# Stick-breaking attention beside weight pieces: another order of a head's steps on ScalarE and VectorE

## The reference

```python
z = einsum(q, k) / sqrt(128)                       # queries of block n, keys 0..(n+1)*128-1
ln = where(before, log_sigmoid(-z), 0)             # before: strictly causal
within = ln @ tri_within                           # reverse exclusive sums inside a 128-key chunk
after = sums of later chunks
w = where(before, exp(z + ln + within + after), 0)
out = w @ v
yb = out @ w_branch_b                              # later: gate_a * ya + gate_b * yb, then w_out
```

## Time and profile before

| | |
|---|---|
| median of three runs | 3065.51 us |
| the profiled execution | 3064.16 us, span 3062.4 us |
| PE busy | 2972.5 us, 97% |
| DVE busy | 1933.2 us, 63% |
| ACT busy | 1523.7 us, 50% |
| mean granted clock of PE | 0.99 |
| DMA | 178 GB/s mean |

### The profile page before, as it was taken

How to read it: one execution, slowest core, us unless ns; L and a number is a source line. 1 busy time by engine, 2 the same in 40 slices (tenths; PEclk the granted TensorE clock), 3 DMA queues, 4 the chain that set the end, 5 groups by cost and what they waited for, 6 DMA issues and landing times. The chain is left out here.

```text
span 3062.4 us, 49424 instructions
## 1 busy us (share of the span) xinstructions
PE 2972.5 (97%) x17246; PEld 2590.4 (85%) x17246; DVE 1933.2 (63%) x2197; ACT 1523.7 (50%) x1897; POOL 265.4 (9%) x217
## 2 busy tenths in 40 slices
PE   7999999999999999999999998999799999999979
PEld 6788888988888888888888887988688888888867
DVE  6487665556665656556656665565777567657664
ACT  4485554444544444444544456444466455545544
POOL 3010011102101010000200000001300000010131
PEclk9999999999999999999999999999899999999989
DMA  7555557665566666665665544655365666656544
GB/s 213 161 160 171 160 169 219 183 179 180 187 195 186 192 192 188 190 189 181 195 186 176 165 152 141 188 168 176 118 188 179 192 192 187 186 185 188 173 130 158
DMA packets 544862, 544.80 MB, mean 178 GB/s; under 512 B 17032, under 2 KB 543880, under 8 KB 544752
## 3 DMA queue, kind: packets, MB, share of 16 engines
q1 hardware_dynamic: 543200, 539.42, 57.8%
q0 software_dynamic: 1552, 3.97, 0.4%
HBM read 541.23 MB, written 2.10 MB: 177 GB/s over the span
## 5 line engine op out<-in xcount | busy, mean ns | idle before, releaser
L1234 DVE TENSOR_TENSOR w_low<-raw,w_high 128x1024 fp32r<-128x1024 f32 x1024 | 1266.7, 1250 | 867.8 <-ACT w_high L895 861.1
L596 PE MATMUL ps_gemm<-act_a,w_high 128*128 128x512 f32 x4480 | 1584.8, 399 | 43.7 <-DVE w_low L1234 25.8
L895 ACT CAST w_high<-raw 128x1024 fp32r<-128x1024 f32 x1024 | 1056.5, 1044 | 1025.0 <-PE ps_gemm L598 1006.6
L598 PE MATMUL ps_gemm<-act_a,w_low 128*128 128x256 f32 x4640 | 1302.9, 281 | 0.0
L596 PE MATMUL ps_gemm<-act_b,w_high 128*128 128x512 f32 x3264 | 1150.2, 398 | 6.3 <-DVE act_b L1243 4.7
L596 PEld LDWEIGHTS ps_gemm<-act_a,w_high 128*128 128x128 f32 x4480 | 846.4, 189 | 252.0 <-issue 41.4
L598 PE MATMUL ps_gemm<-act_b,w_low 128*128 128x256 f32 x3520 | 984.4, 280 | 0.0
L598 PEld LDWEIGHTS ps_gemm<-act_a,w_low 128*128 128x128 f32 x4640 | 882.4, 190 | 0.1
L596 PEld LDWEIGHTS ps_gemm<-act_b,w_high 128*128 128x128 f32 x3264 | 614.2, 188 | 153.6 <-issue 6.0
L598 PEld LDWEIGHTS ps_gemm<-act_b,w_low 128*128 128x128 f32 x3520 | 665.3, 189 | 0.2
L1268 DVE TENSOR_TENSOR summ<-ps_gemm,bcopy 128x512 f32<-128x512 f32 x228 | 156.0, 684 | 22.0 <-ACT bcopy L911 21.4
(11 more groups left out here) (247 smaller groups left out, 1192.1 us busy)
## 6 DMA issues: line engine op xcount, KB each, us to landing
raw<-in_w_in SPq DMA_DIRECT2D x352, 512.0 KB, 4.3
raw<-in_w_up SPq DMA_DIRECT2D x176, 512.0 KB, 3.5
raw<-in_w_mlp_up SPq DMA_DIRECT2D x128, 512.0 KB, 3.9
raw<-in_w_mlp_down SPq DMA_DIRECT2D x128, 512.0 KB, 4.3
raw<-in_w_down SPq DMA_DIRECT2D x88, 512.0 KB, 4.3
raw<-in_w_out SPq DMA_DIRECT2D x64, 512.0 KB, 4.5
raw<-in_w_branch SPq DMA_DIRECT2D x32, 512.0 KB, 4.5
raw<-in_w_ple_gate SPq DMA_DIRECT2D x32, 512.0 KB, 4.4
```

The source lines that it names most:

```text
L596: nc.tensor.matmul(ps[:, g, t, :], wh[:, at, o:o + P], x, start=first, stop=False, skip_group_check=True)
L598: last = nc.tensor.matmul(ps[:, g, t, 0:S], wl[:, at, o:o + P], high(x), start=False, stop=final, skip_group_check=True)
L895: nc.scalar.copy(wh[:, at, 0:kn * S], raw[:, at, 0:kn * S]).then_inc(high_ready, 1)
L1234: nc.vector.tensor_tensor(wl[:, at, 0:kn * S], raw[:, at, 0:kn * S], wh[:, at, 0:kn * S].bitcast(F32), ALU.subtract).then_inc(split_done, 1)
```

## The change

ACT and DVE do more steps of a head directly one behind another, with fewer pieces and no gate epilogue between them; the fillers move behind the head. The Sigmoid table is loaded ahead of the wait for `scaled` in the epilogues of gates_b0, and the load of the Exp table ahead of the second Exp goes (the set natural_log_exp_and_others, loaded for Ln, holds it). The query of the next head is scaled at the end of a head. On PE the loop's first three pieces stand before the loop and again at its end, which leaves its order of instructions as it was; only the value awaited before mix_b0's even pieces is another.

```diff
+            take(fill, 3)
             for h in range(SLOTS):
-                take(fill, 3)
                 pe.wait_ge(y_high, 20 + h)
...
                                  skip_group_check=True).then_inc(s_o, 1)
+                take(fill, 3)
             take(fill)
...
                 def need_y2(i, j, s):
-                    pe.wait_ge(y_done, 24)
+                    pe.wait_ge(y_done, 24 if j % 2 else 20)
...
                 if k == "gate":
+                    if ph.name == "gates_b0":
+                        nc.scalar.preload_act_table(ACT.Sigmoid)
                     act.wait_ge(scaled, after("scaled", ph, i, j))
...
+            take(fill, 2)
             for h in range(SLOTS):
 
-                take(fill, 3)
                 nc.scalar.preload_act_table_set("natural_log_exp_and_others")
...
                 take(fill, 3)
-                nc.scalar.preload_act_table(ACT.Exp)
                 act.wait_ge(s_logw, h + 1)
                 nc.scalar.activation(w3, w3, ACT.Exp).then_inc(s_w, 1)
                 take(fill, 2)
...
                 nc.scalar.copy(act_a[:, 4 + h, 0:S], PJ[:, 28, :]).then_inc(y_high, 1)
+                take(fill, 3)
             take(fill)
...
-            for h in range(SLOTS):
+            take(fill, 2)
+
+            def scale_q(h):
+
                 dve.wait_ge(y_done, 20 + h)
                 nc.vector.tensor_scalar(PJ[:, 20, :], G[:, h, :], HD2_SCALE, None, ALU.mult).then_inc(s_q, 1)
-                take(fill, 2)
+            scale_q(0)
+            for h in range(SLOTS):
                 dve.wait_ge(s_z, h + 1)
...
                 nc.vector.tensor_copy(PJ[:, 21, :], pm[:, 2, 0:S]).then_inc(s_v, 1)
-                take(fill, 2)
                 dve.wait_ge(s_lnb, h + 1)
...
                 nc.vector.tensor_tensor(w3, z3, pm[:, 1, 0:3 * P], ALU.add).then_inc(s_logw, 1)
-                take(fill, 2)
+                take(fill, 3)
                 dve.wait_ge(y_high, 20 + h + 1)
                 low(act_a[:, 4 + h:5 + h, :], PJ[:, 28:29, :], y_done)
+                if h + 1 < SLOTS:
+                    scale_q(h + 1)
+                take(fill, 3)
             take(fill)
```

## The result

The changed kernel took 3043.14 us (median of 19 runs, 3036.70 to 3057.59), the kernel before on the same chip 3062.87 (19 runs, 3056.04 to 3082.54): ratio 0.9936, 95% interval 0.9921 to 0.9950, a gain of 19.7 us (15 to 24). The forecast was 3050 with a range of 3045 to 3060. The profiled execution has a span of 3043.9 us against 3062.4.

A forecast was written before the change was run, and what follows sets the result against it. TensorE, 97% busy, was taken as the bound, so only its stops and lower clock could be won: -12.9 (stops) + 0.25 (query 0) - 3.1 (clock) = -15.75 us, giving 3050 us against the median; range 3045 to 3060.

The forecast's parts named there:

- the last step of the sum: -15.75 us on the profiled 3064.16 gives 3048.4; 1.35 added for the median of 3065.51 gives 3050 us.
- Steps 1 to 5: ACT and DVE order within a head: PE's stops before suffix sums and output go, head 1 becomes 24.6 us.
- Step 3: Masks on DVE ahead of two w_low: the stop before the suffix sums goes, 1.24 us a head.
- step 5: DVE addition and second Exp ahead of the gate epilogue, no Exp table: stop before output goes, 2.41 us.
- step 1: Gate epilogue on ACT: Sigmoid table loaded before the wait for DVE, so Sigmoid ends by 1833.5.
- Step 7: Scaling of query 0 ahead of the first scores: PE waits for it, +0.25 us once (0 to 0.7).
- Step 8: mix_b0 waits for 20 instead of 24 on even pieces: 0 on both sides.
- Step 9: Loads of raw pieces land in 3.6 us, about 7 us available: ACT does not come to wait for one.
- The clock: Stick-breaking stretch: both falls of the granted clock behind output stops of heads 2 and 3 go, 3.1 us (0 to 3.1).
- the clock falls anyway: Rival: the clock falls at other places of the stretch, giving 3053 us; chance 0.15.
- The rival of the thin cover: Fifth piece's w_low, slack 1.5 us, comes late and PE stops there: gain partly given back, 3057 to 3059; chance 0.20.

The follow-up runs named there:

- experiment with three loads: Three more table loads (3.87 us) per head on ACT ahead of the Ln steps, against the changed kernel; 3057.36 us, ratio 0.9981 to the kernel before.

## Why the prediction fell short

The time lies outside the range though every stop went as forecast. What failed is the last step of the sum, the one that sets it "against the median", and the range that was put on it.

- **Steps 1 to 5, order and stops: right.** Head windows of 24.6 were forecast and measured. The stage gives 16.3 us in the first pair of profiles against 12.9 + 3.1 = 16.0 for stops and clock, and 15.6 by the means of all profiles.
- **How the gain divides over the steps: wrong.** Step 3 gave the masks 1.24 us a head, step 5 the Exp 2.41. Alone, the masks are worth 0.75 us a head (28.44 to 27.7), and the Exp step alone is worth 3.6 to 3.8 (28.44 to 24.88 and 24.63), which is all there is. That the sum of the two held is luck in part: both edits were made, and the second would have done it without the first. The table load ahead of the wait (step 1) had been named as what makes Ln early; it is needless.
- **Step 7: right**, 0.25 us. **Step 8: right**, nothing. **Step 9: right**, ACT waits for no load, though the DMA share rose from 0.48 to 0.55.
- **The clock: right**, and firmer than the chance of 0.15 for "the clock falls anyway" had it: 9 falls in five profiles of before, none in the five of the changed order. A fall costs 1.6 us: the stage is 230.8 with one and 232.5 with two. What the prediction held against it, that the clock stayed up behind the stops of head 1, was chance of that one profile: in the third and fifth it fell there.
- **The term that failed is the base.** The sum of -15.75 us was put on the median of three runs, 3065.51; 71 runs put it at 3062.2. With that base the forecast would have been 3046.4, and the range, moved down by the same 3.3 us, would have held the result.
- **What the sum put at nothing.** The other 3 us to the 3043.4 of all changed runs are the excess of the time over the stage. The prediction let the rest of the program stand as it was, without a reason; the profiles show it to differ by up to 17 us between executions of one kernel (1015.7 to 1032.9 behind the stage), and the cause of the 3 us is not found.
- **The range was too narrow for both.** It came from the bounds of the terms and from three runs 8 us apart. Runs of either kernel have a standard deviation near 6 us. A part of it is the pace of PE's pairs, which differs by 2% and is another in each execution. Another part goes with the clock: 6 of the 52 runs of before with a clock on record have a mean of 0.988 or less, and they are its slowest or nearly so, 3070.1 to 3081.0 us against a mean of 3061.3 for the others. Where in those runs the clock is lost no profile shows.
- **The rival of the thin cover: did not come**, at 1.4 us of cover. The experiment with three loads shows that it was the right place, and that a delay beyond the cover is paid in full.

## What to carry over

When two stops in one loop end with different instructions, don't add their lengths as the worth of two edits: look on each engine for the one block (here a gate epilogue, waited for and with its table) that stands ahead of both chains, and move that first. A step of a latency chain belongs ahead of an epilogue with slack; an activation from another table set between two epilogues costs the epilogues a load too. A forecast of under 1% needs the spread of the base, from more than three runs, in its range before the bounds of its terms.

## What the runs showed of the hardware

- A pair of matmuls (512 and 256 columns, fp32) repeats every 347 or 353 ns with the granted clock at 1.00 and PE busy throughout (809 or 794 matmuls in 140 us). Which of the two holds was seen to change at stops of 0.6 and 0.8 us, and differs between executions of one kernel. Over 200 us it makes 3.5 us.
- The granted clock fell to its lower level once or twice in this stage in each of five profiles with PE standing still for 1.1 and 2.3 us with 7 us of work between, once in a profile behind a stop of 2.7 us alone, and three times in one with stops of up to 4.5 us. It did not fall in it with stops of 0.6 and 1.5 us, 1 us of work between, nor without stops. At 352 us of the first profile it fell while PE was busy.
- ACT's next instruction starts 1.29 us after a table load starts, also where loads follow each other: three more made ACT's busy time of a head 3.8 us more (20.47 against 16.68). A load of the table that was in place already takes its 1.28 us too (the changed kernel's at 1855.55, behind the Sigmoid of 1846.97).
